# Expert lists on one Trainium2 core: eight lists made directly instead of four, the table of the rest behind expert 5, the shared product of tiles 2 and 3 interleaved

## What is computed

```python
scores = jax.nn.sigmoid((x @ router_w).astype(jnp.float32))
_, idx = lax.top_k(scores + router_bias, TOP_K)          # 8 of 64 experts per token
sel = jnp.take_along_axis(scores, idx, axis=-1)
wsel = sel / jnp.sum(sel, axis=-1, keepdims=True) * 2.5
gates = jnp.sum(jax.nn.one_hot(idx, N_EXPERTS) * wsel[..., None], axis=1)
hid = jax.nn.silu(jnp.einsum('nd,edf->nef', x, exp_w_gate)) * jnp.einsum('nd,edf->nef', x, exp_w_up)
routed = jnp.einsum('nef,efd->nd', hid * gates[..., None], exp_w_down)
shared = (jax.nn.silu(x @ shared_w_gate) * (x @ shared_w_up)) @ shared_w_down
```

## Time and profile before

| | |
|---|---|
| median of three runs | 774.55 us (774.33 to 775.37) |
| the profiled execution's own time | 774.54 us |
| its span, first to last instruction | 772.8 us |
| TensorE busy, mean granted clock | 91%, 0.986 |
| VectorE, ScalarE, GpSimd busy | 43%, 29%, 39% |
| moved by DMA | 279.14 MB, mean 361 GB/s |

### The profile page before, as it was taken

How to read it: one execution, slowest core, us unless ns; L and a number is a source line. 1 busy time by engine, 2 the same in 40 slices (tenths; PEclk the granted TensorE clock), 3 DMA queues, 4 the chain that set the end, 5 groups by cost and what they waited for, 6 DMA issues and landing times.

```text
span 772.8 us, 15041 instructions
## 1 busy us (share of the span) xinstructions
PE 705.4 (91%) x5129; PEld 391.6 (51%) x5130; DVE 329.5 (43%) x619; ACT 223.9 (29%) x383; POOL 300.4 (39%) x319
## 2 busy tenths in 40 slices
PE   4999999998999999999999999998799977997894
PEld 3666556453545454555555555544455543553541
DVE  4161668277644433444323343333333334334235
ACT  4033603122143322223222232232223223232221
POOL 0050112014155652446445464555535554364210
PEclk9999999998999999999999999999999999999997
DMA  8997999954689999999999999999999999999952
GB/s 355 425 337 277 374 403 353 388 222 193 243 311 389 365 411 399 382 389 401 391 375 398 392 396 402 384 410 395 409 413 401 397 401 410 399 403 401 399 185 70
DMA packets 59126, 279.14 MB, mean 361 GB/s; under 512 B 18804, under 2 KB 19168, under 8 KB 31681
## 3 DMA queue, kind: packets, MB, share of 16 engines
q1 hardware_dynamic: 36112, 252.72, 80.6%
q0 software_dynamic: 22672, 24.81, 13.2%
q10 hardware_dynamic: 288, 0.92, 0.3%
HBM read 272.96 MB, written 25.52 MB: 386 GB/s over the span
## 4 chain that ended last, share of the span: by engine, by line
PE 75%; DMA 18%; DVE 3%; issue 2%; ACT 1%; SPq 1%; POOL 0%; DVEq 0%; POOLq 0%; ACTq 0%
PE bank L1152 31%; PE bank L1191 15%; DMA gu<-in_exp_w_up 14%; PE bank L911 5%; PE bank L893 4%; PE bank L1014 4%; PE bank L1128 3%; DMA gu<-in_lru_in_w 3%; PE bank L881 2%; PE bank L1169 2%; PE bank L914 1%; PE bank L1254 1%; PE bank L1298 1%; PE bank L1290 1%; PE bank L1124 1%
## 5 line engine op out<-in xcount | busy, mean ns | idle before, releaser
L1152 PE MATMUL bank<-gu,et 128*64 128x256 f32 x2480 | 286.1, 383 | 25.1 <-DMA gu<-in_exp_w_up 21.2
L1152 PEld LDWEIGHTS bank<-gu,et 128*64 128x64 f32 x2480 | 181.4, 138 | 145.1 <-issue 68.4
L581 POOL DMA_INDIRECT acc_rows<-et,idx x62 | 101.1, 1630 | 232.5 <-DVE et L1742 137.7
L1191 PE MATMUL bank<-dn,et 128*64 128x512 f32 x632 | 149.7, 602 | 10.5 <-issue 9.7
L1730 DVE COPY et<-bank 128x256 f32<-128x256 f32 x64 | 27.2, 425 | 248.2 <-PE bank L1169 233.6
L779 ACT ACTIVATE et<-bank 64x512 f32<-64x512 f32 x64 | 37.9, 592 | 261.8 <-PE bank L1152 229.9
L1191 PEld LDWEIGHTS bank<-dn,et 128*64 128x64 f32 x632 | 40.4, 136 | 78.1 <-issue 77.9
L794 ACT ACTIVATE et<-bank,mb 128x512 f32<-128x512 f32 x62 | 42.6, 687 | 112.9 <-PE bank L1191 91.1
L1742 DVE TENSOR_SCALAR et<-bank,mb 128x512 f32<-128x512 f32 x62 | 46.6, 751 | 64.3 <-PE bank L1191 51.4
L1723 DVE TENSOR_TENSOR et<-et 64x512 f32<-64x512 f32 x64 | 67.9, 1060 | 4.2 <-ACT et L780 4.1
L591 POOL DMA_DIRECT2D small<-halfc x48 | 54.6, 1138 | 0.0
(11 more groups left out here) (302 smaller groups left out, 629.3 us busy)
## 6 DMA issues: line engine op xcount, KB each, us to landing
dn<-in_exp_w_down SPq DMA_DIRECT2D x64, 1024.0 KB
gu<-in_exp_w_up SPq DMA_DIRECT2D x63, 1024.0 KB
gu<-in_exp_w_gate SPq DMA_DIRECT2D x62, 1024.0 KB
gu<-in_ada_rest SPq DMA_DIRECT2D x5, 2048.0 KB, 10.1
gu<-in_mix_w SPq DMA_DIRECT2D x3, 2048.0 KB, 13.8
mb<-in_ada_rest SPq DMA_DIRECT2D x3, 2048.0 KB, 11.6
gu<-in_lru_in_w SPq DMA_DIRECT2D x4, 1024.0 KB, 17.4
gu<-in_sgu_in_w SPq DMA_DIRECT2D x2, 2048.0 KB, 19.6
```

The costliest lines, as they stand in the source:

```text
L581: pool.indirect_dma_start(acc_rows[u % 2], bass.IndirectOffsetOnAxis(ap=idx[:, u, 0:1], axis=0), yo[:, u % 2, 0, :], None, bounds_check=2 ...
L1152: mm = pe.matmul(bank[u % 2][64 * c:64 * c + 64, b * FE:(b + 1) * FE], xt[:, b, k % 4, k // 4, :], w[c][:, k * FE:(k + 1) * FE], start=(k ...
L1191: mm = pe.matmul(bank[out[b]][64 * c:64 * c + 64, :], hT[:, b, j, :], dn[:, dslot(u), j * D + c * HALF:j * D + (c + 1) * HALF], start=(j = ...
```

## The change

`FIRST` becomes 8: eight lists are made directly, in two groups of four, and the table serves 56 experts. The rank scan moves behind the first lists (`ranked`). POOL makes the first two pieces from the bf16 mask as soon as that is there. PE does tiles 2 and 3 of the shared product step by step, with the lists 0 to 3 after the third step, the lists 4 to 7 and the turn of expert 0 before the last. SP loads expert 3's gate half and the first 1280 columns of expert 4's into freed space after four steps, the rest after the last. The table's `moving` operands go into the space of expert 4's operands, so they wait for its gate-up; the table stands around the down product of expert 4, behind gate-up 5, and indices 8 and 9 wait for it. DVE makes the one-hots in four batches of two beside experts 0 to 3. The spatial gate takes tiles 1 and 2 together, 128 columns per head, and tile 3 in bank 7.

```diff
-FIRST = 4
+FIRST = 8
...
-        BATCHES = ((0, 2), (2, 4), (4, 8))
+        BATCHES = ((0, 2), (2, 4), (4, 6), (6, 8))
...
+        def mv(k):
+            home = late[:, D + 480 * (k - 5):D + 480 * (k - 4)] if k in (5, 6) else xTf[:, 480 * (k % 7):480 * (k % 7 + 1)]
...
-                    sync.wait_ge(*((s["mod_ready"], 6), (s["wout_ready"], 5), (s["wout_ready"], 5), (s["sh_ready"], 3))[g])
+                    sync.wait_ge(*((s["mod_ready"], 6), (s["wout_ready"], 5), (s["wout_ready"], 5), (s["counted"], 1))[g])
...
+                if isinstance(g, int) and g == SLOTS - 1:
+                    sync.wait_ge(s["sh_ready"], 2)
+                    sync.dma_start(guf[sl][:, 0:KT * FE], eg[e]).then_inc(ld_gu[sl], 16)
+                    sync.dma_start(xTf[:, 0:4 * T], eg[SLOTS][:, 0:4 * T]).then_inc(ld_shared_gu, 16)
+                    sync.wait_ge(s["sh_ready"], 4)
...
+            pool.wait_ge(s["mask_done"], 1)
+            pool.tensor_tensor(parts[:, :, 0:2, :], mask_b.rearrange("p t (o e) -> p t o e", o=1).to_broadcast([P, 3, 2, NE]),
+                               tokp.rearrange("p t (c o) -> p t c o", o=1).to_broadcast([P, 3, 2, NE]), ALU.mult).then_inc(s["pieces"], 1)
             pool.wait_ge(s["route_step"], 9)
...
                     if not (first and u == 0):
                         y1(r, i if u else i - 1, (u - 1) % U)
+                    if first and r == 0 and u == 5:
+                        spread_table(0)
...
+            pair = (tp_wait("s0"), tp_wait("s1"))
+            for g in range(8):
+                mm = pe.matmul(pair[g // 4][:, (g % 4) * P:(g % 4 + 1) * P].rearrange("p (t n) -> p t n", t=2), wT[:, g, :],
+                               vv[:, 0:2, g * 64:(g + 1) * 64], start=True, stop=True)
...
+            pe.wait_ge(s["prj_evac"], len(PRJ))
+            for g in range(8):
+                mm = pe.matmul(tp_bank("s2")[0:64, g * 64:(g + 1) * 64], wsT[0:64, g, :], vv[0:64, 2, g * 64:(g + 1) * 64], start=True, stop=True)
...
-                    if first and r == 0 and u == 0:
-                        table(0, 0)
-                    if first and r == 0 and u == 1:
-                        table(0, 2)
+                    listing = r == 0 and isinstance(i, int) and i == 1 and u == 1
...
-                    if first and r == 0 and u == 0:
+                    if listing:
+                        table(0, 0)
                         table(0, 1)
                     if before is not None:
                         down(r, i if u else i - 1, (u - 1) % V, before)
+                    if listing:
+                        table(0, 2)
+                        table(0, 3)
...
-                    tile_product(bank[5], 1, gu[SH_SLOT], 2 * FE, range(3))
-                    lists()
-                    tile_product(bank[5], 1, gu[SH_SLOT], 2 * FE, range(3, KT)).then_inc(s["sh_ready"], 1)
-                    shared_gu(2)
-                    pe.wait_ge(s["flags"], 1)
+                    for k in range(KT):
+                        for t in (1, 2):
+                            mm = tile_product(bank[4 + t], t, gu[SH_SLOT], 2 * FE, range(k, k + 1))
+                            if k == KT - 1 or (k, t) == (3, 2):
+                                mm.then_inc(s["sh_ready"], 1)
+                        if k == 2:
+                            lists(0, SLOTS)
+                        if k == KT - 2:
+                            lists(SLOTS, FIRST)
+                            pe.wait_ge(s["flags"], 1)
+                            turn_x(0, 0, 0, is_full(0, 0, 0))
...
                 if h == 0 and r == 0:
                     dve.wait_ge(s["pieces"], 6)
+                    dve.wait_ge(s["gu_done"], SLOTS + 1)
...
+                    front = first and r == 0
+                    if front and u == 6:
+                        index(0, 1, 0)
                     if not (first and u == 0):
                         ht(*before)
-                    if first and r == 0 and u == 1:
-                        table_sums(0)
+                    if front and u == 5:
+                        moving(0, 2)
+                    if front and u == 6:
+                        index(0, 1, 1)
...
                     hidden(r, i, u)
-                    if late and u == 0:
-                        moving(0, 2)
...
+                    if front and u == 4:
+                        moving(0, 0)
+                        moving(0, 1)
+                    if front and u == 5:
+                        moving(0, 3)
                     if not (first and u == 0 or last and u == U - 1):
                         y0(*before)
+                    if front and u < 4:
+                        one_hots(0, u)
+                    if front and u == 5:
+                        table_sums(0)
...
-                    first_lists()
+                    first_lists(0)
                     counts()
-                    first_sums()
+                    first_sums(0)
                     for u in range(AHEAD + 1):
                         index(0, 0, u)
-                    one_hots(0, 0)
-                    moving(0, 0)
+                    first_lists(1)
                     shared_hidden(0)
-                    one_hots(0, 1)
-                    moving(0, 1)
+                    ranked()
+                    first_sums(1)
+                    xt0(0, 0, 0)
                     shared_hidden(1)
                     shared_hidden(2)
-                    xt0(0, 0, 0)
-                    one_hots(0, 2)
```

More of the change, by code:

```diff
@@ L366, in load_gu @@
                 sl = gslot(g, u)
-                if not (isinstance(g, int) and g == SLOTS + 1):
+                if isinstance(g, int) and g == SLOTS - 1:
[3 more added lines that the diff above has]
+                    sync.wait_ge(s["sh_ready"], 4)
+                elif not (isinstance(g, int) and g == SLOTS + 1):
                     sync.dma_start(guf[sl][:, 0:KT * FE], eg[e]).then_inc(ld_gu[sl], 16)
@@ L776, in gates @@
                 act.wait_ge(s["gu_done"], e + 1)
-                if not (isinstance(e, int) and e == 0):
+                if isinstance(e, int) and e == 0:
+                    act.wait_ge(s["sh_hid"], 3)
+                else:
                     act.wait_ge(s["hid_ready"], e)
@@ L1096, in table, with lists @@
                     for t, (t0, m) in enumerate(TILES):
-                        mm = pe.matmul(bank[7][:, 0:PC * NE], oh(k)[0:m, t, :], mv(r, k)[0:m, t].rearrange("p c e -> p (c e)"),
+                        mm = pe.matmul(bank[7][:, 0:PC * NE], oh(k)[0:m, t, :], mv(k)[0:m, t].rearrange("p c e -> p (c e)"),
                                        start=(k == 0 and t == 0), stop=(k == TOP - 1 and t == 2))
                     mm.then_inc(s["tb_mm"], 1)
-            def lists():
+            def lists(e0, e1):
                 pe.wait_ge(s["pieces"], 6)
                 pe.wait_ge(s["sc_done"], 3)
-                for e in range(FIRST):
+                for e in range(e0, e1):
                     pe.wait_ge(s["ohd_done"], e + 1)
@@ L1618, in _, with ranked @@
                 dve.tensor_tensor(pos[0:n, t, :], b[0:n, t * NE:(t + 1) * NE], shift[0:n], ALU.add).then_inc(s["route_step"], 1)
-            dve.wait_ge(s["route_step"], 13)
+            dve.wait_ge(s["route_step"], 12)
+            def ranked():
+                link(dve.tensor_tensor_scan(rank.rearrange("p t e -> p (t e)"), restart.rearrange("p t e -> p (t e)"),
+                                            mask.rearrange("p t e -> p (t e)"), 0.0, ALU.mult, ALU.add))
+                dve.tensor_tensor(rank, rank, mask, ALU.mult).then_inc(s["route_step"], 1)
+                dve.wait_ge(s["route_step"], 13)
             def counts():
@@ L1653, in shared_sum, with first_lists @@
                 dve.tensor_tensor(x[0:n, t, cols], x[0:n, t, cols], y, ALU.add).then_inc(s["pre_done"], 1)
-            def first_lists():
+            def first_lists(g):
                 dve.wait_ge(s["out_small"], 64)
-                for e in range(FIRST):
+                for e in range(SLOTS * g, SLOTS * g + SLOTS):
                     dve.tensor_tensor(ohd(e), iota_s[:, 0:P].rearrange("p (o n) -> p o n", o=1).to_broadcast([P, 3, P]),
@@ L1753, in body @@
                         shared_turned(half // 2)
-                    late = first and r == 0 and u < 2
-                    if not (late or last and u >= U - AHEAD - 1):
+                    if not (front and u in (4, 5) or last and u >= U - AHEAD - 1):
                         index(r, i + (u + AHEAD + 1) // U, (u + AHEAD + 1) % U)
```

104 lines of the change are left out of this document (49 added, 55 removed).

## The result

The changed kernel takes 776.83 us in the median of ten runs (773.27 to 778.63); the kernel before, on the same chip, 774.52 us (773.64 to 775.37). The ratio is 1.0029 with an interval from 1.0018 to 1.0040: 2.3 us slower, where 2.1 us less had been forecast. The profiled execution took 776.59 us (span 774.9 us, mean granted clock 0.987).

The account below looks back on a forecast made before the run. DMA loads of expert weights were taken to bound the kernel, held near 336 us by TensorE. TensorE's terms sum to -1.2 us at expert 10, plus 0.9 of backlog: -2.1 us from 774.5, so 772.4 us, range 768.3 to 777.2.

Parts of the forecast that it names:

- What bounds the kernel: Whole kernel: expert weight loads set the end, TensorE second; near 336 us loads wait for slots TensorE frees.
- The loads around 223.17: SP's expert weight loads issued around 223.17 us: would come 7.9 us earlier, the gate load near 215.3.
- The backlog of 0.9 us: Near 336 us: loads can run ahead of PE by 0.9 us more before the engines run dry (0.8 to 3.4).
- The spatial gate: Spatial gate on PE's path: 32 instructions for 48, wide ones 2.1 us, narrow 1.6; saves 1.2 us (0 to 1.6).
- Tiles 2 and 3: Shared product and first lists: PE's 2.29 us wait goes, full clock follows; a step of both tiles costs 1.41 us.
- Gather 0: Inside the shared product: second part takes 4.0 us, PE waits 1.6 us, gate-up 0 starts 3.3 us earlier.
- the first experts without the table: Between gate-up 0 and 1, without the table hiding ACT's passes: PE turns and waits, +1.4 us (1.2 to 1.8).
- rival B: Clock falls again while PE waits for gather 0, costing 2.7 us: 775.1 us, no change that can be told; chance 0.23.
- The table behind expert 5 and gather 8: Behind gate-up 5: table's 4.83 us return; gather 8 takes 8 us, stall 1.9 us in all (0 to 6).
- Sum: PE from expert 10 on: -1.2 - 3.3 + 1.4 + 1.9 = -1.2 us; with 0.9 more for the loads, -2.1 us.
- Rival C: Early loads delay gather 0 by 3 us, clock falls: +3.6, 778.1 us; decided by expert 0's turn after 194; chance 0.17.

Follow-up runs that it names:

- changed, second profile: The changed kernel profiled once more without any edit; one execution, 778.32 us.
- gate alone: Kernel before with only the new spatial gate (32 instructions for 48, third product in bank 7): 773.65 us against 774.15, ratio 0.9986.
- copy first: Changed kernel, with ScalarE copying expert 1's transposed tokens before the two gate passes of expert 0: 775.11 us, ratio 1.0014.
- no early loads: Changed kernel, with expert 3's gate half and expert 4's first 1280 columns waiting until the shared product is done: 774.53 us, ratio 1.0002.
- ten lists: Changed kernel with lists of ten experts made directly instead of eight, so indices 8 and 9 don't wait for the table: 772.63 us, ratio 0.9977.
- three edits: Changed kernel with lists of ten, expert 1's copy ahead of the gate passes and no early loads: 771.41 us, ratio 0.9963.
- cover: Kernel with the three edits, second group of lists made between gate-up 0 and 1 instead of inside the shared product: 769.14 us, ratio 0.9930.
- fewer changes of tile: Kernel with the lists as cover, tiles 2 and 3 of the shared product changing places 6 times instead of 16: 767.92 us, ratio 0.9916, the fastest.
- early loads back: Fastest version (lists as cover, six changes of tile) with the changed kernel's early loads of experts 3 and 4 put back: 772.21 us, ratio 0.9964.
- old gate: Fastest version (without early loads) with the spatial gate of the kernel before: 769.72 us, ratio 0.9938.

## Why the prediction was wrong

All profiled executions together, in us; the last column is the fourth less the second:

| kernel | gate-up 10 starts | lowest DMA share, 310:320 and 320:330 | own time | difference |
|---|---|---|---|---|
| before | 273.60 | 1.03 | 774.54 | 500.9 |
| changed | 275.81 | 0.91 | 776.59 | 500.8 |
| changed, second profile | 277.88 | 0.85 | 778.32 | 500.4 |
| gate alone | 272.41 | 1.02 | 774.20 | 501.8 |
| copy first | 273.75 | 0.86 | 774.82 | 501.1 |
| no early loads | 273.16 | 0.87 | 774.17 | 501.0 |
| ten lists | 270.94 | 0.99 | 770.62 | 499.7 |
| three edits | 269.72 | 0.98 | 770.30 | 500.6 |
| cover | 269.04 | 0.99 | 769.53 | 500.5 |
| fewer changes of tile | 267.39 | 0.99 | 768.68 | 501.3 |
| early loads back | 273.08 | 0.99 | 773.97 | 500.9 |
| old gate | 269.44 | 1.00 | 770.61 | 501.2 |

- **What bounds the kernel**: right in kind. The loads are held to TensorE between 310 and 330 us, as the prediction said near 336, and the 3.0 us taken out of the hole are worth nothing behind a late TensorE. The time follows gate-up 10 within 1.2 us over a range of 10 us, and two runs part the loads from TensorE: without the early loads the loads start later, TensorE arrives earlier and the time falls; with them back in the fastest version it is the other way round. Where the share stays near 1, the loads and TensorE move together, and these runs don't tell which of the two sets the end there.
- **The loads around 223.17** came 4.75 us earlier (218.42) and not 7.9, since TensorE's gate-ups, which free their slots, were late by the rest.
- **The backlog of 0.9 us** was sized too high. The kernel before has no dip, yet the four executions with one stand at the same difference, 500.4 to 501.1 against 500.9. So no slack of 0.9 us shows; how small it was can't be told, since executions without a dip scatter from 499.7 to 501.8.
- **The spatial gate**: -1.2 forecast, -1.73 measured. The term for the wide products, 2.1 us, was right (119.44 to 121.43); the narrow ones took 1.07 instead of 1.6.
- **Tiles 2 and 3**: no wait and full clock, as forecast. Not seen: that a step of both tiles costs 1.64 us instead of 1.41 when they alternate. That made the product 1.8 us longer (8 x 0.23), hidden in the changed kernel by the wait for gather 0.
- **Gather 0**: 4.1 us from the start of its second part to TensorE (188.84 to 192.99), as taken, but with another cause: undisturbed it needs at most 3.0 (188.82 to 191.80), and the early loads cost the rest. That part also started at 188.84 instead of 187.9 (189.1 less 1.2), because POOL's first instruction took 2.30 us beside the masks. This late start is the 0.95 us by which gate-up 0 comes at 195.35 instead of 194.4; the cost of the early loads was already inside the 4.0 us taken.
- **The step that failed: two waits were priced by their length alone, "+1.4 us" for the first experts without the table and "1.9 us in all" before expert 8; the half clock behind them was put at nothing.** The wait before gate-up 1 was 1.83 us, at the upper bound given, but the clock fell behind it and gate-up 1 took 1.7 us longer. Between gate-up 0 and 2 this is +3.6 instead of +1.4. The prediction had the fall of the clock only as rival B, at the wait for gather 0. There the granted clock from 190 to 200 us was 1.00 in the first profile and 0.83 in the second, so it can happen there too.
- **The table behind expert 5 and gather 8**: net +1.9 was about right from gate-up 2 to 10 (+2.1), by luck. Gather 8 needed 9.9 us (248.79 to 258.67) instead of 8, the stall was 2.60 us, and half clock behind it cost 1.2 us in the down product and 0.5 in gate-up 8, which nothing in the term stood for. Against it, TensorE's waits in the kernel before, 0.92 us ahead of expert 10's turn and 0.26 and 0.36 us ahead of those of experts 8 and 9, went away, and the stretch from gate-up 2 to 6, with the table in it, became 4.1 us longer and not 4.83. The lists of ten show the price of the whole: with them and a full clock in gate-up 1, 4.9 us.
- **Sum**: at gate-up 10 +2.2 instead of -1.2. The half clock in two places, 1.7 + 1.7 us, is as large as the difference; the other misses (gate -0.5, gather 0 +1.5, copy +0.5, and -1.5 for the stall, the table and the waits that went away) cancel.
- **Rival C** took place in part: its mechanism cost 1.2 us here and shows in full once the product is shorter, with the 2.29 us wait and the half clock (early loads put back). Its point of decision, the turn of expert 0 after 194, was not reached (192.99).

The spread of the changed kernel's runs, 773.27 to 778.63, would fit one stretch of half clock more or less, each some 2 us; the two profiles differ by one. That all runs differ for this reason was not shown.

## What to carry to other kernels

Price a wait of TensorE with the half-speed stretch that can follow it: here a wait of 1.83 us cost 1.7 us more behind it in both profiles of the changed kernel, and nothing more in another version. Work that "costs" time on the bounding engine may be the cover of a copy or a gather; when it is moved away, move other work that is needed later, here the second lists, into its place. And before a load is started early to fill idle engines, ask what small transfer, on which an engine waits, runs in that gap: 1.7 MB of early loads cost 4.3 us through a gather.

## What was not expected of the hardware

- **POOL's gather instruction takes longer beside VectorE's masks.** It took 2.30 us beside four masks, 3.24 beside six, 1.26 with none, and about 1.03 us in later gathers. In the first two cases it ended 1.0 us after the last mask (188.53 and 187.51; 189.66 and 188.64). VectorE's last masks, changed kernel and three edits:

```profile
186.02 1.49 DVE L1688 TENSOR_TENSOR mb<-iota_s,mb 128x384 bf16<-128x384 f32 x3
...
187.62 1.02 DVE L1691 TENSOR_TENSOR sh<-iota_s,mb 128x384 bf16<-128x384 f32 x2
```

The Trainium skill ("SBUF — State Buffer", Who interferes with whom) says that two-input operations of VectorE contend with GpSimd instructions that read SBUF. The gather, which reads its index, agrees with that: 2.30 and 3.24 against 1.26 us. The page also infers that such operations don't hold up the making of descriptors. Here the whole instruction of the gather was held up, and the measurement decides; which part of it waits was not seen.
- **A change between tiles 2 and 3 cost TensorE 0.17 us**, 1.7 us for ten changes fewer at a clock of 1.00.
- **The same wait of TensorE is followed by the lower clock or not.** Between 170 and 300 us it fell behind every wait of 2.29 us and more (2.29 before the lists or for gather 0, 2.59 to 2.70 before expert 8); late in the kernel before, a wait of 2.52 us that ended at 715.72 was followed by a granted clock of 1.00. It stayed full behind 1.66 (changed) and 1.85 (copy first) for gather 0, and fell behind 1.74 (changed, second profile). It fell behind 1.83 for the copy (changed, both profiles) and stayed full behind the same 1.83 when the wait 10 us ahead of it was 0.47. And it fell once, with the gate alone, behind waits of 0.43 and 0.16 us. So no length of a wait is shown here that decides it.
